# Splitting the first gate chunk of the light experts in halves, and moving two small writes on VectorE

## The reference

```
x_rows = xt[row_tok]                                  # rows sorted by expert
hdn = jax.nn.silu(xb @ w1[e]) * (xb @ w3[e])          # 1024 -> 512, gate and up
y   = hdn @ w2[e]                                     # 512 -> 1024, down
out = out.at[row_tok].add(y * row_w[:, None])         # weighted, added to h
```

## Time and profile before

| | before |
|---|---|
| median of 3 runs | 1173.18 us |
| profiled execution, and its span | 1172.78 us, 1171.0 us |
| TensorE busy with matmuls (PE), with weight loads (PEld) | 1115.4 us (95%), 860.2 us (73%) |
| VectorE (DVE), ScalarE (ACT), GpSimd (POOL) busy | 879.3 us, 695.1 us, 338.9 us |
| low parts of the experts' chunks (L2054), 190 | 434.0 us, 2291 ns each |
| high parts of the experts' chunks (L2050), 190 | 362.5 us, 1909 ns each |
| weight transfers of 1 MB, 192 | 19.6 us from issue to landing (median) |

### The profile page before, as it was taken

The page is one execution under the profiler, slowest core; times in us unless marked ns, Lnnn a source line. Parts: engine busy times, 40 slices in busy tenths (PEclk is TensorE's granted clock), DMA queues, the critical chain, the costliest instruction groups (busy, mean ns, idle before and its releaser), DMA issues.

```text
span 1171.0 us, 17312 instructions
## 1 busy us (share of the span) xinstructions
PE 1115.4 (95%) x5838; PEld 860.2 (73%) x5839; DVE 879.3 (75%) x1298; ACT 695.1 (59%) x958; POOL 338.9 (29%) x394
## 2 busy tenths in 40 slices
PE   6999999999999989999699999999999999999997
PEld 5877887767777678888567777777777777777775
DVE  4424323666566788888679999999999999999995
ACT  5425202544455544434347777777777788888884
POOL 1211102321111221222463242323424245444211
PEclk9998999999999999999789999999999999999999
DMA  8130302110200263342589999999999999999992
GB/s 323 47 108 1 108 1 72 35 65 28 99 28 18 91 186 140 131 177 95 206 319 385 373 393 380 380 395 372 392 377 378 389 376 385 398 391 385 395 390 66
DMA packets 66912, 271.66 MB, mean 232 GB/s; under 512 B 12757, under 2 KB 19481, under 8 KB 42393
## 3 DMA queue, kind: packets, MB, share of 16 engines
q1 hardware_dynamic: 57000, 245.32, 53.8%
q0 software_dynamic: 6384, 19.14, 7.1%
q10 hardware_dynamic: 3456, 6.29, 1.4%
HBM read 246.74 MB, written 26.48 MB: 233 GB/s over the span
## 4 chain that ended last, share of the span: by engine, by line
PE 80%; DVE 10%; ACT 5%; issue 2%; POOL 2%; DMA 1%; ACTq 0%; POOLq 0%; SPq 0%; DVEq 0%
PE main_pm L693 13%; PE main_score L693 7%; PE main_score L2084 5%; PE main_score L2086 5%; PE main_score L2085 5%; DVE main_w_low L2054 4%; PE main_score L754 3%; PE main_pt L2086 3%; PE main_pt L2084 3%; PE main_po L2086 3%; PE main_po L2084 3%; PE main_pt L2085 3%; PE main_po L2085 3%; ACT main_w_high L2050 2%; PE main_pt L2096 2%
## 5 line engine op out<-in xcount | busy, mean ns | idle before, releaser
L2054 DVE TENSOR_TENSOR main_w_low<-w_raw,main_w_high 128x2048 fp32r<-128x2048 f32 x190 | 434.0, 2291 | 38.8 <-ACT main_w_high L2050 36.9
L2050 ACT CAST main_w_high<-w_raw 128x2048 fp32r<-128x2048 f32 x190 | 362.5, 1909 | 68.5 <-PE main_score L2086 52.2
L1953 POOL DMA_INDIRECT main_xg<-xn_dram,main_token x32 | 79.0, 2468 | 275.4 <-DVE main_token L1926 264.5
L2084 PE MATMUL main_score<-main_w_high,main_hT_high 128*96 128x512 f32 x256 | 102.6, 401 | 1.1 <-DVE main_hT_low L2345 0.6
L2086 PE MATMUL main_score<-main_w_high,main_hT_low 128*96 128x512 f32 x256 | 100.7, 393 | 0.0
L2085 PE MATMUL main_score<-main_w_low,main_hT_high 128*96 128x512 f32 x256 | 100.3, 392 | 0.0
L693 PE MATMUL main_pm<-slot_high,xh 128*128 128x512 f32 x208 | 87.7, 422 | 2.1 <-DVE slot_low L1404 2.1
L693 PE MATMUL main_pm<-slot_low,xh 128*128 128x512 f32 x208 | 82.9, 398 | 0.0
L693 PE MATMUL main_pm<-slot_high,xl 128*128 128x512 f32 x208 | 82.8, 398 | 0.0
L1998 POOL DMA_INDIRECT out<-main_y,main_dest x31 | 50.0, 1614 | 89.3 <-ACT main_y L2010 60.7
L1055 ACT ACTIVATE main_prob<-main_score,main_nmax 128x128 f32<-128x128 f32 (+7 forms) x64 | 47.6, 744 | 33.4 <-DVE main_nmax L1463 32.5
(11 more groups left out here) (375 smaller groups left out, 2615.9 us busy)
## 6 DMA issues: line engine op xcount, KB each, us to landing
w_raw<-in_moe_w SPq DMA_DIRECT2D x192, 1024.0 KB, 19.6
slot_raw<-in_w_in SPq DMA_DIRECT2D x12, 1024.0 KB, 7.3
main_x<-in_x SPq DMA_DIRECT2D x8, 512.0 KB, 11.2
slot_raw<-in_w_out SPq DMA_DIRECT2D x4, 1024.0 KB, 6.8
main_hx<-in_x SPq DMA_DIRECT2D x8, 512.0 KB, 3.9
out<-main_hx SPq DMA_DIRECT2D x8, 512.0 KB, 2.6
xn_dram<-main_xn SPq DMA_DIRECT2D x8, 512.0 KB, 2.8
gr_dram<-main_stage ACTq DMA_DIRECT2D x8, 256.0 KB, 2.0
```

The lines of the kernel that those rows point to most:

```text
L1953: nc.gpsimd.indirect_dma_start(xg[u][0:slots], None, s["xn2_dram"], bass.IndirectOffsetOnAxis(token[u][0:slots, 0:1], 0), bounds_check=bou ...
L2050: nc.scalar.copy(wh[slot(c, e)][:], raw[u][c // 2][:, c % 2, :]).then_inc(w_high, 1)
L2054: nc.vector.tensor_tensor(wl[slot(c, e)][:], raw[u][c // 2][:, c % 2, :], wh[slot(c, e)][:].bitcast(F32), ALU.subtract).then_inc(w_low, 1)
L2084: nc.tensor.matmul(out, x_hi, w_hi, start=start, stop=False)
```

## The change

Two things are moved in the experts' part. For each light expert but the first (numbers 19 to 31), the high part of gate chunk 0 is written in two halves of 1024 columns, each with its own count, and the low part likewise, so that the second engine may begin on the first half. And from expert 1 on, `dve_targets` moves from its place behind the low part of chunk 4 to the end of VectorE's order for the expert, behind the low part of the next expert's chunk 1. The new count needs a semaphore, which comes from the front: the two loads that `gain_in` counted are now counted by `head_in`, whose waits go from 128 to 160.

```diff
-            sp.dma_start(out_gain[:, i:i + 1], a[n].rearrange("a k -> k a")).then_inc(gain_in, 16)
+            sp.dma_start(out_gain[:, i:i + 1], a[n].rearrange("a k -> k a")).then_inc(head_in, 16)
...
+    w_half = sem("w_high_half_ready")
...
+    def high_by_half(act, e, r, u):
+        act.wait_ge(raw_in[u][0], 16 * (r + 1))
+        act.wait_ge(chunk_used, number(e, 0) - 2)
+        for half in range(2):
+            w = slice(half * D, half * D + D)
+            nc.scalar.copy(wh[slot(0)][:, w], raw[u][0][:, 0, w]).then_inc((w_half, w_high)[half], 1)
+
+    def low_by_half(dve, e, u):
+        for half in range(2):
+            if half == 0:
+                dve.wait_ge(w_half, e - HEAVY)
+            else:
+                dve.wait_ge(w_high, number(e, 0) + 1)
+            w = slice(half * D, half * D + D)
+            done = nc.vector.tensor_tensor(wl[slot(0)][:, w], raw[u][0][:, 0, w], wh[slot(0)][:, w].bitcast(F32),
+                                           ALU.subtract)
+        done.then_inc(w_low, 1)
...
-        if more:
+        if more and light[1]:
+            high_by_half(act, e + 1, pair(r, j, 1), 1 - u)
+        elif more:
             high(act, e + 1, pair(r, j, 1), 1 - u, 0)
...
-        elif not (last and j >= 2):
-            dve_targets(dve, e + 2, r + 1, (j + 2) % 4)
...
-            low(dve, e + 1, 1 - u, 0)
+            if light[1]:
+                low_by_half(dve, e + 1, 1 - u)
+            else:
+                low(dve, e + 1, 1 - u, 0)
...
+        if some(e, 1) and not (last and j >= 2):
+            dve_targets(dve, e + 2, r + 1, (j + 2) % 4)
```

More of the change, by code:

```diff
@@ L352, in stage_front @@
     rel_in, bias_in, z_in = sem("rel_in"), sem("bias_in"), sem("z_in")
-    gain_in, head_in = sem("gain_in"), sem("head_in")
+    head_in = sem("head_in")
     rel_out, filled, rel_step, lam_step = sem("rel_out"), sem("filled"), sem("rel_step"), sem("lam_step")
@@ L1431, in lam_part @@
             if stage_ == 0:
-                dve.wait_ge(head_in, 128)
+                dve.wait_ge(head_in, 160)
                 for i in range(2):
@@ L1437, in lam_part @@
                 nc.vector.tensor_reduce(lsum[:], lprod[:], AX.X, ALU.add).then_inc(lam_step, 1)
-                dve.wait_ge(head_in, 128)
+                dve.wait_ge(head_in, 160)
                 nc.vector.tensor_scalar(s["gain_q"][:], graw[:, 0:1], DDK ** -0.5 * DDK ** 0.5, None, ALU.mult)
                 nc.vector.tensor_scalar(s["gain_k"][:], graw[:, 1:2], DDK ** 0.5, None, ALU.mult)
-                dve.wait_ge(gain_in, 32)
+                dve.wait_ge(head_in, 160)
                 nc.vector.tensor_scalar(out_gain[:, 0:1], out_gain[:, 0:1], GDV ** 0.5, None, ALU.mult)
```

## The result

The change makes the kernel slower by 0.24%: a median of 1174.12 us (1171.06 to 1176.64, 20 runs) against 1171.81 us (1169.55 to 1173.31, 20 runs) for the kernel before, ratio 1.0024, 95% interval 1.0017 to 1.0031. Forecast were 1173.0 us and, as likeliest by far (0.74), no change that can be told. The difference is small, but the runs tell it, and it is put together otherwise than forecast: the heavy stage lost more, the light stage gained almost nothing.

A forecast was written before the change was run, and what follows sets the result against it. TensorE was taken to bound the heavy stage, a loop of waits through ScalarE, VectorE and TensorE the light one. From 1172.78 us, -2.0 (light) and +2.2 (heavy) gave 1173.0 us, range 1169.6 to 1177.0.

The forecast's parts named there:

- Which stage is bound by what: TensorE bounds the heavy stage; a loop of waits through ScalarE, VectorE and TensorE, 16.90 us per expert, the light one.
- The heavy stage: Moved writes stand ahead of `hd` and delay its transposes at 17 products: 2.2 us lost, bounds 0 and 5.0.
- The price t: Time the writes of `wrow` and `dest` add at their new place: 0.20 us, bounds 0 and 0.36.
- The light stage: Ten steps, 19 to 28, gain 0.23 us each; with losses in steps 29 to 31, -2.0 us in all.
- The closest that a load follows its releaser is 0.06: Smallest distance in us from a releasing instruction to TensorE's weight load, applied to the load for the down matmul.
- this path has 0.41 us to spare: Light steps: `hT_low` ends 0.47 us before the down load, so it may come 0.41 us later at no cost.
- The two steps without a token list: Light steps 29 and 30, where the load already closely follows `hT_low`: 0.12 us lost each.
- The sum: Whole kernel: 1172.78 - 2.0 + 2.2 = 1173.0 us, the sign of the change left open.
- The rest at nothing: The moved writes' later reads, their scatter wait, SyncE's issues and the front's waits were all taken to cost 0.
- Gate decides: Rival: writes ride free in pauses, light stage gains, capped by weights at 3.6 us, heavy loses nothing: 1169.2 us; chance 0.13.
- Full durations: Rival: the two writes cost 0.36 us wherever VectorE is waited for, net +4.9 us: 1177.7 us; chance 0.16.
- Weight stream: Rival: weight transfers pace the light stage, so no light gain and the heavy loss of 2.2 stays: 1175.0 us; chance 0.09.

The follow-up runs named there:

- e2: Against the kernel before: only the two writes of `dve_targets` moved, gate chunk 0 left whole; 1174.06 us, ratio 1.0029.
- e3: The changed kernel with the two writes of heavy experts back at their old place; 1172.62 us, ratio 1.0010 to the kernel before.
- e4: The changed kernel with TensorE's wait for `hT_low` put last of three ahead of down chunk 2; 1175.26 us, ratio 1.0034 to the kernel before.
- e1: The changed kernel with the halves kept and the two writes back behind chunk 4; 1187.03 us, ratio 1.0105 to the kernel before.
- e8: The changed kernel with heavy writes at the old place, light ones between mask and chunk 1, `hT_low` wait last; 1169.50 us, ratio 0.9979 to the kernel before.
- e6: The changed kernel with heavy writes directly behind `hd`, one expert too early; 1262.36 us, ratio 1.0790 to the kernel before.

## Why the prediction was wrong, step by step

- **Which stage is bound by what: right.** TensorE in the heavy stage, the loop through ScalarE, VectorE and TensorE in the light one; the halves removed VectorE's idle 0.48 us, and the hidden values came next, as said.
- **The heavy stage: right mechanism, term mis-sized.** For 17 products, "13 x 0.11 + 4 x 0.20 = 2.2 us"; measured +2.8 us (e2 and e3 agree). The price t was taken as 0.20 from the old place, where the low part of the tokens follows; ahead of `hd` it is 0.24 (`dest` to `hd` 0.11 in place of 0.07). With that, the prediction's own formula gives 13 x 0.15 + 4 x 0.24 = 2.9; the spare 0.09 us and the count of four without it were right.
- **The light stage: the step that failed** is "The closest that a load follows its releaser is 0.06", and what hangs on it, that "this path has 0.41 us to spare". That row stands at `hd`. At the down matmul, inside the loop, two more waits are queued behind the one for `hT_low`, and the closest distance is 0.21; e4 shows that moving these two ahead takes 0.10 off the step. Outside the loop, with the same two waits behind it, the distance is 0.05, so the queue is not the whole of it; what the loop adds no run isolates. The delays were also larger: ScalarE's two halves hold the next instruction 1.91 us (1002.47 - 1000.56) in place of 1.81, so 0.10 for 0.07, and chunks 1 and 2 start 2.41 apart (1007.95 - 1005.54), so 0.12 for 0.11 over half of the 4.58 of the earlier trace rows. 0.47 - 0.21 - 0.10 - 0.12 = 0.04 us a step, measured 0.06, where 0.23 was forecast. The two steps without a token list, forecast to lose 0.12 us each, lose 0.12 and 0.36: ahead of the second stand the three writes of the last list (0.44 us). In all -0.3 us in place of -2.0.
- **The sum.** +2.8 - 0.3 = +2.5 us by the traces, and 0.35 more outside the span, which the prediction took to stay as it was; +2.3 by the medians, with an interval of 2.0 to 3.6. Forecast was +0.2.
- **"The rest at nothing": wrong in kind.** The wait of the writes for an earlier scatter was indeed met sooner at the later place; what it was worth there was not asked. With the halves at the old place and nothing else done, the wait costs 9 to 24 us (e1).
- **The rivals.** Gate decides: no, the hidden values do. Full durations: no, 0.24 and 0.20; the 0.36 us of two writes are not seen. Weight stream: no, e8 runs 16.62 us a step with the same transfers.

## What to carry to other kernels

Read a path's spare time at the instruction that will wait, in the code that will run there: here a loop with further waits queued behind the releasing one kept 0.21 us, where the closest pairs elsewhere showed 0.05 and 0.06. An instruction that is moved takes its own waits along, so look up when their releasers land at the old place and at the new: a margin of 2 us that no wait shows can be what the other half of the change lives on. Put small writes where their engine idles for another one, not directly ahead of what the full engine waits for.

## What had not been expected of the hardware

A gather that takes 0.99 us on GpSimd while VectorE is idle (e6) and 2.4 beside one subtraction took 4.5, 5.1, 7.4 and 9.5 us beside a VectorE that was late by 0.10 us at the least, and ended each time 0.85 to 0.87 us behind the end of a VectorE instruction. Lateness of 0.24 us on one engine thus grew to 9 to 24 us in e1, with two engines each waiting on the other. Why a gather is let in or held up there is open.
